# Where the mLSTM normalizer's column sum is made: on TensorE from four score tiles, or on VectorE first

## The chip, the cores and the metric

The kernel runs on one core of one Trainium2 chip. The metric is the device time of one execution in microseconds. The engines are named TensorE (PE, with its weight loads PEld), VectorE (DVE), ScalarE (ACT), GpSimd (POOL) and SyncE (SP, which starts the transfers).

## The reference, cut to what matters

Two transformer-like blocks run one after the other on 512 tokens of width 1024. The second block holds an mLSTM layer ("matrix memory") with 4 heads. In the kernel each head is computed over all 512 tokens at once and not chunk by chunk. For one head, with q and k of width 256 and v of width 512:

```
W[t, s]  = exp(F[t] - F[s] + i[s] - m[t])      for s <= t, else 0
Sm[t, s] = (q[t] . k[s]) * W[t, s]
num[t]   = sum over s of Sm[t, s] * v[s]
den[t]   = sum over s of Sm[t, s]
h[t]     = num[t] / max(|den[t]|, exp(-m[t]))
```

`den` is the normalizer. After it come an output gate, a layer norm over the 512 channels of the head, a skip term and a gate `silu(z)`, and then the output product.

## The kernel before, in words

All work is on tiles of 128 partitions by 512 tokens. Weights come in panels of 128 x 1024 through a ring of four buffers: SyncE loads `raw`, ScalarE rounds it to `w_hi` (line 1295), GpSimd computes `w_lo = raw - w_hi` (line 749). `dense` multiplies such a panel by a split input in three products (lines 778, 779, 784). The results go round the PSUM banks 0 to 3; tile t is in bank t % 4. `bank_ready(t)` makes TensorE wait until every earlier tile of that bank was taken, and `tile_taken(pe, t)` until tile t itself was. Banks 4 to 7 are for single sums and scores; `free` waits for one of them. Every engine works through its own instruction list in the order written, and semaphores join them. Nothing is scheduled at run time.

One head (`m_attend`) goes like this. The places that matter below are in this order on each engine.

- TensorE: products for q and k. Then v in two halves (lines 1079 to 1081), both halves into the tiles t0+4 to t0+7, which fill banks 0 to 3. Between the halves come the score products (line 1096), into banks 4, 5 and 6. After the second half of v comes the normalizer (line 1106): for each block n of 128 source tokens a product of a matrix of ones with the score tile `st` of that block, into bank 4. Block n only concerns the tokens from 128n on, so the four products have 512, 384, 256 and 128 columns. Then come the four numerator groups (line 1117, one for each 128 channels, d = 0 to 3) into the tiles t0+8 to t0+11, again banks 0 to 3, each with the same four widths. Then `dense(p0 + 4, t0 + 12)` for the first z tile, the product for the mean (line 1125), further z tiles, and the product for the variance (line 1131). The operands of lines 1096, 1106, 1117, 1125 and 1131 are plain fp32, and the trace holds two records for each such product.
- ScalarE: copies of q and k, the exponentials, the copies of the four v tiles to `mv` (line 1638), one panel rounding (line 1295), and then `den = |bank 4|` (line 1641). `den` is shown as `hf` in the trace.
- VectorE: the score tiles `st` (line 2233); then `max(den, exp(-m))` (line 2242), its reciprocal (line 2243), four products of it with the output gate `og` (line 2246), and four products of `og` with the numerator banks (line 2251). Each of the latter sets a numerator bank free. Between them the sum over channels is built up in `rstd` (lines 2255 and 2258). The mean product reads that sum.

The first numerator group has these two waits ahead of it:

```
bank_ready(t)
if d == 0:
    for n in range(NT):
        tile_taken(pe, t0 + 4 + n)
```

The tiles t0+4 to t0+7 are the v tiles, which ScalarE takes at line 1638.

Of the kernel before, what the change touches and what calls it, by code (L numbers as in the profile page):

```python
# [20 lines left out]
ALU = mybir.AluOpType  # L21
ACT = mybir.ActivationFunctionType

P = 128
S = 512
NT = S // P
# [188 lines left out]
def two_blocks(nc, A, out, stop=None):  # L215
    ctx = ExitStack()
    with ctx:
        def sem(name):
            return ctx.enter_context(nc.semaphore(name))
# [25 lines left out]
        ones = sb("ones", [P, P], F32)  # L245
# [7 lines left out]
        rstd = sb("rstd", [P, S], F32)  # L253
# [83 lines left out]
        st = sb("st", [P, 1280], F32, a)  # L337
# [69 lines left out]
        bank = [ctx.enter_context(nc.psum_tensor(f"bank{b}", [P, S], F32)) for b in range(8)]  # L407
# [102 lines left out]
        st_made = sem("st_made")  # L510
        den_done = sem("den_done")
        num_done = sem("num_done")
        absden_made = sem("absden_made")
        hsum_made = sem("hsum_made")
        msq_used = sem("msq_used")
        mean_done = sem("mean_done")
# [238 lines left out]
        def _(pe):  # L755
# [90 lines left out]
            for g in range(GG):  # L846
                mm = pe.transpose(bank[7][:, g * P:(g + 1) * P], ws[:, g, :], ident[:])
# [210 lines left out]
            def m_attend(i):  # L1058
                def free(b, n):
                    aux_released(pe, b, AUX_M[b] + n + i * M_AUX[b])  # L1060
                p0, t0 = M_BP[i], M_BT[i]
                for z in range(2):
                    dense(p0 + z, t0 + 2 * z, hi=xc_hi, lo=xc_lo, kt=4, width=2,
                          need=(lambda k: pe.wait_ge(xcs_made, i * MT + (k + 1))) if z == 0 else None)

                for z in range(2):
                    p = p0 + 2 + z
                    panel_split(pe, p)
                    if z == 0:
                        pe.wait_ge(xm_made, (i + 1) * MT)  # L1070
                    for n in range(NT):
                        if z == 0:
                            bank_ready(t0 + 4 + n)
                        dst = bank[(t0 + 4 + n) % RING][:, z * 256:(z + 1) * 256]
                        c = slice(n * P, (n + 1) * P)
                        for k in range(MT):
                            wh = w_hi[:, p % RING, k * 256:(k + 1) * 256]
                            wl = w_lo[:, p % RING, k * 256:(k + 1) * 256]
                            pe.matmul(dst, xm_hi[:, k, c], wh, start=(k == 0), stop=False, skip_group_check=True)  # L1079
                            pe.matmul(dst, xm_hi[:, k, c], wl, start=False, stop=False, skip_group_check=True)  # L1080
                            mm = pe.matmul(dst, xm_lo[:, k, c], wh, start=False, stop=(k == MT - 1),  # L1081
                                           skip_group_check=True)
                    mm.then_inc(panel_done[p % RING], 1)
                    if z == 0:

                        for e in range(MQ):
                            tile_taken(pe, t0 + e)
                            tile_taken(pe, t0 + 2 + e)
                        free(4, 0)
                        free(5, 1)  # L1090
                        free(6, 0)
                        for n in range(NT):
                            b, at = score_bank(n)
                            width = S - n * P
                            for e in range(MQ):
                                mm = pe.matmul(b[:, at:at + width], mk[:, e, n * P:(n + 1) * P],  # L1096
                                               mq[:, e, n * P:S], start=(e == 0 and n != 3), stop=(e == MQ - 1),
                                               skip_group_check=True)
                            mm.then_inc(scores_done, 1)

                place_st = [0, 512, 896, 1152]
                free(4, 1)
                for n in range(NT):
                    pe.wait_ge(st_made, i * NT + (n + 1))
                    w = S - n * P
                    mm = pe.matmul(bank[4][:, n * P:S], ones[:], st[:, place_st[n]:place_st[n] + w],
                                   start=(n == 0), stop=(n == NT - 1), skip_group_check=True)
                mm.then_inc(den_done, 1)
                for d in range(MT):
                    t = t0 + 8 + d  # L1110
                    bank_ready(t)
# [4 lines that stand above are left out]
                        w = S - n * P  # L1116
                        mm = pe.matmul(bank[t % RING][:, n * P:S], mv[:, n, d * P:(d + 1) * P],  # L1117
                                       st[:, place_st[n]:place_st[n] + w], start=(n == 0), stop=(n == NT - 1),
                                       skip_group_check=True)
                    mm.then_inc(num_done, 1)  # L1120

                dense(p0 + 4, t0 + 12)
                free(5, 2)
                pe.wait_ge(hsum_made, (i + 1) * (MT - 1))
                pe.matmul(bank[5][:], ones_m[:], rstd[:], start=True, stop=True).then_inc(mean_done, 1)
                dense(p0 + 5, t0 + 13)
                if i < MH - 1:
                    dense(p0 + 6, t0 + 14)
                free(6, 1)
                pe.wait_ge(msq_used, (i + 1) * MT)  # L1130
                pe.matmul(bank[6][:], ones_m[:], rstd[:], start=True, stop=True).then_inc(var_done, 1)
                if i == MH - 1:
                    dense(p0 + 6, t0 + 14)
                dense(p0 + 7, t0 + 15)
# [648 lines left out]
        def _(dve):  # L1783
# [430 lines left out]
            def m_attend(i):  # L2214
# [22 lines left out]
                dve.wait_ge(st_made, (i + 1) * NT)  # L2237
                for b in (4, 5, 6):
                    dve.sem_inc(aux_free[b], 1)

                dve.wait_ge(aux_free[4], AUX_M[4] + 2 + i * 2)
                link(dve.tensor_tensor(den, den, enm, ALU.max))
# [4 lines left out]
                for d in range(MT):  # L2247
                    t = t0 + 8 + d
                    dve.wait_ge(num_done, i * MT + (d + 1))
                    dve.wait_ge(den_used, i * MT + (d + 1))  # L2250
                    dve.tensor_tensor(og[:, d, :], bank[t % RING][:], og[:, d, :], ALU.mult)\
                       .then_inc(taken[t % RING], 1)
                    tile_taken(dve, t)
                    if d == 1:
                        dve.tensor_tensor(rstd[:], og[:, 0, :], og[:, 1, :], ALU.add).then_inc(hsum_made, 1)
                    elif d:
                        dve.wait_ge(hsum_made, i * (MT - 1) + (d - 1))
                        dve.tensor_tensor(rstd[:], rstd[:], og[:, d, :], ALU.add).then_inc(hsum_made, 1)
# [273 lines left out]
```

## Time and profile before

| | |
|---|---|
| median of 3 runs | 1710.41 us (1708.61 to 1710.64) |
| the profiled execution | 1710.67 us, span in the trace 1709.0 us |
| mean granted TensorE clock | 0.986 of full speed |
| TensorE busy | 1661.2 us, 97% of the span |
| VectorE, ScalarE, GpSimd busy | 864.2, 823.9, 715.2 us |
| chain that ended last | PE 87%, DVE 7%, ACT 4% |
| the four heads' normalizer products | first at 998.1 us, last head's at 1386.6 us |

Times in the trace count from the start of the span. A row of a timeline has the start, the length, the engine, the line and what was written from what; equal neighbours are merged with their count. A bracket says how long the engine had been idle before and what ended that. TensorE's records overlap, because a product begins before the one ahead of it has drained; so the distance between two starts is the cost of a product, and its record's length is more than that.

### The profile page before, as it was taken

To read this page: it belongs to the slowest core of one execution; us is meant where nothing else is said; L and a number is where in the kernel's file an instruction comes from. 1 tells how busy PE (TensorE), PEld (TensorE's weight loads), DVE (VectorE), ACT (ScalarE), POOL (GpSimd) and SP (SyncE) were. 2 spreads that over 40 slices of the span, in tenths; PEclk is the share of its full clock that TensorE was granted. 3 is DMA by queue.
4 is the path that set the end of the run, shared out by engine and by line. 5 is a ranking of instruction groups with operands and counts; after the bars stand their busy time and mean duration, and the time that the engine had idled before them with its cause. 6 is when DMAs were issued, how large, how long until landed. Compare 5 with 4: busy or idle time off the path is not lost.

```text
span 1709.0 us, 21678 instructions
## 1 busy us (share of the span) xinstructions
PE 1661.2 (97%) x7693; PEld 1362.4 (80%) x7693; DVE 864.2 (51%) x1356; ACT 823.9 (48%) x1091; POOL 715.2 (42%) x933
## 2 busy tenths in 40 slices
PE   6989999989999999999999999999999998999997
PEld 5878888878888888888887777877877876788875
DVE  4466666641113311111145757457447447688676
ACT  5366777653334423222246645445434435665664
POOL 5542333326666555555566535635635632000000
PEclk8989999999999999999999999999999999999999
DMA  6322212213333333333333222322422412322311
GB/s 175 99 62 62 61 49 61 62 38 93 99 104 99 99 99 98 94 96 96 98 98 90 72 60 75 111 62 75 111 61 68 116 52 79 97 88 66 107 56 59
DMA packets 251095, 142.94 MB, mean 84 GB/s; under 512 B 6161, under 2 KB 249618, under 8 KB 251026
## 3 DMA queue, kind: packets, MB, share of 16 engines
q1 hardware_dynamic: 251026, 142.00, 28.9%
q8 instruction: 45, 0.74, 0.2%
q14 instruction: 24, 0.20, 0.0%
HBM read 139.89 MB, written 2.10 MB: 83 GB/s over the span
## 4 chain that ended last, share of the span: by engine, by line
PE 87%; DVE 7%; ACT 4%; issue 1%; DMA 0%; SPq 0%; DVEq 0%; ACTq 0%
PE bank L778 22%; PE bank L779 22%; PE bank L784 22%; PE bank L1117 2%; PE bank L903 2%; PE bank L769 2%; PE bank L771 2%; PE bank L770 2%; ACT w_hi L1295 1%; PE bank L1096 1%; PE bank L1081 1%; PE bank L1080 1%; PE bank L1079 1%; PE bank L916 1%; DVE xT L2054 1%
## 5 line engine op out<-in xcount | busy, mean ns | idle before, releaser
L749 POOL TENSOR_TENSOR w_lo<-raw,w_hi 128x256 fp32r<-128x256 f32 x896 | 704.7, 819 | 711.6 <-ACT w_hi L1295 711.5
L1295 ACT ACTIVATE w_hi<-raw 128x1024 fp32r<-128x1024 f32 x264 | 277.5, 1056 | 538.2 <-PE bank L784 479.8
L778 PE MATMUL bank<-h_hi,w_hi 128*128 128x512 f32 x1252 | 501.3, 400 | 0.0
L779 PE MATMUL bank<-h_lo,w_hi 128*128 128x512 f32 x1252 | 490.1, 391 | 0.0
L784 PE MATMUL bank<-h_hi,w_lo 128*128 128x512 f32 x1252 | 309.3, 389 | 0.0
L778 PEld LDWEIGHTS bank<-h_hi,w_hi 128*128 128x128 f32 x1252 | 236.5, 189 | 56.3 <-issue 7.5
L779 PEld LDWEIGHTS bank<-h_lo,w_hi 128*128 128x128 f32 x1252 | 236.6, 189 | 52.8 <-issue 4.3
L784 PEld LDWEIGHTS bank<-h_hi,w_lo 128*128 128x128 f32 x1252 | 235.0, 188 | 48.8
L2054 DVE TENSOR_TENSOR xT<-xT,bank 128x512 f32<-128x512 f32 x103 | 68.3, 685 | 208.1 <-PE bank L784 156.9
L2079 DVE SCALAR_TENSOR_TENSOR fr<-bank,rstd 128x512 f32<-128x512 f32 x32 | 22.1, 692 | 133.6 <-PE bank L784 127.9
L778 PE MATMUL bank<-f_hi,w_hi 128*128 128x512 f32 x224 | 87.1, 389 | 0.0
L779 PE MATMUL bank<-f_lo,w_hi 128*128 128x512 f32 x224 | 87.1, 389 | 0.0
L2038 DVE TENSOR_TENSOR gated<-sg,bank 128x512 f32<-128x512 f32 x16 | 11.0, 689 | 110.3 <-PE bank L784 108.8
L903 PE MATMUL bank<-qk 128*128 128x64 f32 x448 | 56.1, 286 | 8.5 <-ACT vT L1396 8.5
L1380 ACT ACTIVATE ee<-ee 128x512 f32<-128x512 f32 x72 | 44.6, 630 | 37.0 <-DVE ee L1952 35.7
L903 PEld LDWEIGHTS bank<-qk 128*128 128x128 f32 x448 | 54.8, 203 | 9.5 <-issue 6.9
L784 PE MATMUL bank<-f_hi,w_lo 128*128 128x512 f32 x224 | 55.3, 389 | 0.0
L779 PEld LDWEIGHTS bank<-f_lo,w_hi 128*128 128x128 f32 x224 | 42.1, 188 | 8.8
L784 PEld LDWEIGHTS bank<-f_hi,w_lo 128*128 128x128 f32 x224 | 42.0, 188 | 8.7
L778 PEld LDWEIGHTS bank<-f_hi,w_hi 128*128 128x128 f32 x224 | 42.0, 188 | 8.7
L2331 DVE TENSOR_TENSOR w_lo<-raw,w_hi 128x1024 fp32r<-128x1024 f32 x40 | 48.7, 1217 | 0.0
L1998 DVE COPY_PREDICATED sd<-mask,bank 128x256 f32<-128x256 uint8 x56 | 29.5, 527 | 27.4 <-PE bank L903 21.5
(415 smaller groups left out, 2705.3 us busy)
## 6 DMA issues: line engine op xcount, KB each, us to landing
raw<-in_w_ff SPq DMA_DIRECT2D x64, 512.0 KB, 4.1
raw<-in_w_in SPq DMA_DIRECT2D x56, 512.0 KB, 3.8
raw<-in_m_w_in SPq DMA_DIRECT2D x48, 512.0 KB, 3.9
raw<-in_r_w_in SPq DMA_DIRECT2D x24, 512.0 KB, 3.9
raw<-in_m_w_out SPq DMA_DIRECT2D x16, 512.0 KB, 3.5
raw<-in_r_w_out SPq DMA_DIRECT2D x16, 384.0 KB, 3.1
raw<-in_w_up_b SPq DMA_DIRECT2D x8, 512.0 KB, 4.2
raw<-in_w_out SPq DMA_DIRECT2D x8, 512.0 KB, 4.2
```

The lines of the kernel that those rows point to most:

```text
L749: ins = pool.tensor_tensor(w_lo[:, s, part], raw[:, s, part], w_hi[:, s, part].bitcast(F32), ALU.subtract)
L769: pe.matmul(dst, w_hi[:, s, c], hi[:, k, :], start=(k == 0), stop=False)
L770: pe.matmul(dst, w_hi[:, s, c], lo[:, k, :], start=False, stop=False)
L771: mm = pe.matmul(dst, w_lo[:, s, c], hi[:, k, :], start=False, stop=(k == kt - 1))
L778: pe.matmul(dst, w_hi[:, s, c], hi[:, k, :], start=(k == 0), stop=False)
L779: pe.matmul(dst, w_hi[:, s, c], lo[:, k, :], start=False, stop=False)
L784: mm = pe.matmul(dst, w_lo[:, s, c], hi[:, k, :], start=False, stop=(k == kt - 1))
L903: mm = pe.matmul(dst, qk[:, m - 1, c], right, start=True, stop=True, skip_group_check=True)
L1295: act.activation(w_hi[:, p % RING, :], raw[:, p % RING, :], ACT.Copy).then_inc(hi_ready[p % RING], 1)
L1380: act.activation(ee[:, l % 3, :], ee[:, l % 3, :], ACT.Exp).then_inc(decay_made, 1)
L2054: dve.tensor_tensor(xT[:, j, :], xT[:, j, :], bank[t % RING][:], ALU.add).then_inc(taken[t % RING], 1)
L2331: dve.tensor_tensor(w_lo[:, q, :], raw[:, q, :], w_hi[:, q, :].bitcast(F32), ALU.subtract).then_inc(lo_ready[q], 1)
```

## The change

On VectorE, once the four score tiles are made, three additions put the tiles n = 1, 2 and 3 together with tile 0 for the tokens from 128 on (384, 256 and 128 columns) and write the sum to `rstd`, a buffer that is free at that point. They sit ahead of `max(den, ...)` in VectorE's list.

On TensorE the four products with ones go away. Two take their place: one over the 128 columns of tile 0 that no other tile reaches, and one over the 384 columns of `rstd`. These two stand behind the first numerator group (d = 0) and no longer ahead of it. TensorE now waits for all four score tiles at once, and for the three additions ahead of the two products.

VectorE gets one further wait, for `den_done`, ahead of its first channel sum, since that one overwrites `rstd`.

```diff
--- before.py
+++ after.py
@@ -510,7 +510,7 @@
         st_made = sem("st_made")
         den_done = sem("den_done")
         num_done = sem("num_done")
-        absden_made = sem("absden_made")
+        stsum_made = sem("stsum_made")
         hsum_made = sem("hsum_made")
         msq_used = sem("msq_used")
         mean_done = sem("mean_done")
@@ -1099,13 +1099,7 @@
                             mm.then_inc(scores_done, 1)
 
                 place_st = [0, 512, 896, 1152]
-                free(4, 1)
-                for n in range(NT):
-                    pe.wait_ge(st_made, i * NT + (n + 1))
-                    w = S - n * P
-                    mm = pe.matmul(bank[4][:, n * P:S], ones[:], st[:, place_st[n]:place_st[n] + w],
-                                   start=(n == 0), stop=(n == NT - 1), skip_group_check=True)
-                mm.then_inc(den_done, 1)
+                pe.wait_ge(st_made, (i + 1) * NT)
                 for d in range(MT):
                     t = t0 + 8 + d
                     bank_ready(t)
@@ -1118,6 +1112,12 @@
                                        st[:, place_st[n]:place_st[n] + w], start=(n == 0), stop=(n == NT - 1),
                                        skip_group_check=True)
                     mm.then_inc(num_done, 1)
+                    if d == 0:
+                        free(4, 1)
+                        pe.wait_ge(stsum_made, (i + 1) * (NT - 1))
+                        pe.matmul(bank[4][:, 0:P], ones[:], st[:, 0:P], start=True, stop=False, skip_group_check=True)
+                        pe.matmul(bank[4][:, P:S], ones[:], rstd[:, P:S], start=False, stop=True,
+                                  skip_group_check=True).then_inc(den_done, 1)
 
                 dense(p0 + 4, t0 + 12)
                 free(5, 2)
@@ -2237,6 +2237,12 @@
                 dve.wait_ge(st_made, (i + 1) * NT)
                 for b in (4, 5, 6):
                     dve.sem_inc(aux_free[b], 1)
+                dve.tensor_tensor(rstd[:, P:S], st[:, P:S], st[:, place_st[1]:place_st[1] + S - P],
+                                  ALU.add).then_inc(stsum_made, 1)
+                for n in range(2, NT):
+                    dve.wait_ge(stsum_made, i * (NT - 1) + (n - 1))
+                    dve.tensor_tensor(rstd[:, n * P:S], rstd[:, n * P:S], st[:, place_st[n]:place_st[n] + S - n * P],
+                                      ALU.add).then_inc(stsum_made, 1)
 
                 dve.wait_ge(aux_free[4], AUX_M[4] + 2 + i * 2)
                 link(dve.tensor_tensor(den, den, enm, ALU.max))
@@ -2252,6 +2258,7 @@
                        .then_inc(taken[t % RING], 1)
                     tile_taken(dve, t)
                     if d == 1:
+                        dve.wait_ge(den_done, i + 1)
                         dve.tensor_tensor(rstd[:], og[:, 0, :], og[:, 1, :], ALU.add).then_inc(hsum_made, 1)
                     elif d:
                         dve.wait_ge(hsum_made, i * (MT - 1) + (d - 1))
```

## Rows read from the trace of the kernel before

**Rows 1.** The page: busy time of each engine, and the chain that ended last.
```profile
PE 1661.2 (97%) x7693; PEld 1362.4 (80%) x7693; DVE 864.2 (51%) x1356; ACT 823.9 (48%) x1091; POOL 715.2 (42%) x933
...
PE 87%; DVE 7%; ACT 4%; issue 1%; DMA 0%; SPq 0%; DVEq 0%; ACTq 0%
```

**Rows 2.** Timeline, TensorE, head 0: start us, length us, engine, line, operation, tiles, [idle].
```profile
997.98 0.28 PE L1081 MATMUL bank<-w_hi,xm_lo 128*128 128x256 f32 x1
998.10 2.32 PE L1106 MATMUL bank<-st,ones 128*128 128x512 f32 x8
1000.50 8.87 PE L1117 MATMUL bank<-st,mv 128*128 128x512 f32 x32
...
1014.82 0.59 PE L1125 MATMUL bank<-rstd,ones_m 128*128 128x512 f32 x1
```

**Rows 3.** Timeline, ScalarE, head 0.
```profile
998.29 2.06 ACT L1638 ACTIVATE mv<-bank 128x512 f32<-128x512 f32 x4 [4.39 <-PE bank L1081]
1000.22 1.08 ACT L1295 ACTIVATE w_hi<-raw 128x1024 fp32r<-128x1024 f32 x1
1001.17 0.62 ACT L1641 ACTIVATE hf<-bank 128x512 f32<-128x512 f32 x1
```

**Rows 4.** Timeline, TensorE's weight loads, head 0.
```profile
1003.60 1.49 PEld L1117 LDWEIGHTS bank<-st,mv 128*128 128x128 f32 x7 [0.24 <-issue]
...
1005.76 1.49 PEld L1117 LDWEIGHTS bank<-st,mv 128*128 128x128 f32 x7 [0.24 <-issue]
...
1009.23 0.19 PEld L778 LDWEIGHTS bank<-h_hi,w_hi 128*128 128x128 f32 x1
```

**Rows 5.** Timeline, VectorE, head 0.
```profile
992.61 0.62 DVE L2233 TENSOR_TENSOR st<-ww,bank 128x256 f32<-128x256 f32 x2 [0.37 <-PE bank L1096]
1001.82 0.83 DVE L2242 TENSOR_TENSOR hf<-hf 128x512 f32<-128x512 f32 x1 [8.59 <-ACT hf L1641]
...
1008.49 1.41 DVE L2251 TENSOR_TENSOR og<-bank,og 128x512 f32<-128x512 f32 x2
...
1012.59 0.69 DVE L2258 TENSOR_TENSOR rstd<-rstd,og 128x512 f32<-128x512 f32 x1
```

**Rows 6.** Waits from 975 to 1500 us: waiter, releaser, us, times, longest.
```profile
DVE hf L2242 <- ACT hf L1641: 34.4, 4, 8.6
...
ACT mv L1638 <- PE bank L1081: 17.6, 4, 4.4
```

**Rows 7.** Groups by shape, VectorE, 950 to 1500 us: busy us, mean ns, idle.
```profile
L2288 DVE TENSOR_TENSOR og<-og,rstd 128x512 f32<-128x512 f32 x16 | 15.0, 938 | 0.1
...
L2233 DVE TENSOR_TENSOR st<-ww,bank 128x384 f32<-128x384 f32 x4 | 2.2, 554 | 0.9 <-PE bank L1096 0.9
```

**Rows 8.** Timeline, GpSimd, head 0.
```profile
1001.38 3.23 POOL L749 TENSOR_TENSOR w_lo<-raw,w_hi 128x256 fp32r<-128x256 f32 x4 [4.58 <-ACT w_hi L1295]
```

**Rows 9.** Stretches: us; busy us (instructions) of PE, PEld, DVE, ACT, POOL; clock; DMA.
```profile
1422.90:1424.80 1.90, 0.00 (x0) 0.00 (x0) 1.81 (x3) 0.62 (x2) 0.00 (x0) 1.00 0.00 0
1425.00:1428.00 3.00, 3.00 (x8) 2.10 (x8) 2.93 (x4) 1.39 (x2) 2.17 (x3) 0.51 0.09 25
...
967.73:969.64 1.91, 1.91 (x6) 0.66 (x5) 1.91 (x3) 1.71 (x3) 1.91 (x4) 1.00 0.20 37
971.10:974.40 3.30, 3.30 (x9) 2.55 (x8) 3.30 (x4) 2.70 (x4) 3.30 (x4) 0.50 0.49 128
1054.80:1056.70 1.90, 1.90 (x5) 0.66 (x4) 1.83 (x4) 0.14 (x1) 0.00 (x0) 1.00 0.04 9
1057.00:1060.40 3.40, 3.40 (x16) 2.78 (x16) 3.26 (x6) 2.29 (x4) 1.52 (x2) 1.00 0.00 0
```

**Rows 10.** Timeline, TensorE, head 3.
```profile
1410.86 1.10 PE L1131 MATMUL bank<-rstd,ones_m 128*128 128x512 f32 x2 [1.01 <-DVE rstd L2284]
```

## The prediction

> **What bounds the kernel now.** I read the page first. TensorE is busy 97% of the span and carries 87% of the chain that ended last [rows 1]. So work taken off TensorE looks like time won, and that is the case for this change. But a share over the whole span hides what ends each wait in the stretch that is edited, so I went on to the timelines of one head, engine by engine. The four heads repeat each other: the wait of ScalarE for the v products and the wait of VectorE for the normalizer each occur four times, at 17.6 / 4 = 4.4 us and 34.4 / 4 = 8.6 us [rows 6].
>
> In TensorE's timeline [rows 2] the last v product ends at 998.26 (997.98 + 0.28), the normalizer runs from 998.10 to 1000.42, and the numerator begins at 1000.50. It looks like one unbroken stream. ScalarE's timeline tells what it hides: the four v copies start at 998.29, when the last v product has ended, and end at 1000.35 [rows 3]. By the code the first numerator group waits for all four copies. It starts 0.15 us after the last of them. So the start of the numerator is set by ScalarE, and the old normalizer fills exactly the 2.24 us (998.26 to 1000.50) in which TensorE has nothing else that it may do. Its cost on TensorE is close to nothing.
>
> The second thing to see is who waits for the normalizer. ScalarE copies it at 1001.17, directly behind a panel rounding that began at 1000.22 [rows 3]. It was complete at 1000.42, so it was ScalarE's list that held the copy. VectorE had been idle for 8.59 us when the copy released it at 1001.82. From there its list runs to 1012.59 + 0.69 without a pause [rows 5]. In that list the first numerator bank is set free at 1009.19 (the two records of line 2251 take 1.41 us together from 1008.49, so one takes 0.70). TensorE's next step, the first z tile, needs that bank, and its weight load starts at 1009.23 [rows 4]. TensorE and VectorE meet there within 0.04 us. VectorE's list has no slack at this point, and it is the normalizer that starts the list.
>
> **The change part by part.**
>
> *Products removed and put in.* A numerator group has the same four widths as the old normalizer and takes 1005.76 - 1003.60 = 2.16 us [rows 4]. That is ten blocks of 128 columns. The new pair has 128 + 384 columns, four blocks: 2.16 x 4 / 10 = 0.86 us. Nominal saving: 1.30 us a head, 5.2 us for four. None of it is on the path: what is removed lay under the v copies (they end at 1000.35 whatever TensorE does), and what is put in lies behind the first group, where nothing covers it. So TensorE's own list gets 0.86 us longer between 1000.50 and the z tile: it would arrive at 1009.23 + 0.86 = 1010.09.
>
> At this place the Trainium skill has a rule that speaks against the change (TensorE: Matmul & The Clock Gate, Part 2, Step-by-step): only weight loads are pulled ahead; the products themselves stay in program order. By it TensorE can't do the new pair during the 2.24 us, although its operands are there. If it could, the normalizer would be ready as early as now and the time would stay near the old one.
>
> *The additions on VectorE.* The trace has no addition of 384, 256 or 128 columns from SBUF alone. From below: the score tile of 384 columns takes 0.55 us [rows 7], so three shorter or equal ones take at most 1.7 us at that rate. From above: a 512-column product of two SBUF tiles takes 0.94 us on average where other engines are at work [rows 7], three take 2.8 us. They start at 993.23, when the last score tile is done [rows 5], and end between 994.9 and 996.1. TensorE asks for them at about 1002.7. The cover is 6.6 us or more, inside an idle stretch of 8.59 us; I take nothing. GpSimd may work at the same time; even if all three additions held it up in full, 2.8 us fit into its idle 4.58 us ahead of its next split [rows 8]. No transfer and no queue of SyncE is touched. The additional wait of VectorE for `den_done` comes after work that itself needed the normalizer, so it is always met: nothing.
>
> *The wait for all four score tiles at once.* They are done at 993.23, 5 us before TensorE gets there: nothing.
>
> *The move.* This is what costs. Now: the normalizer's last product ends at 1000.42 and the copy starts at 1001.17. After: the first numerator group starts at 1000.50 as before, the pair begins at 1002.66, its stream ends at 1003.52, and the last record drains 0.16 us later (as 2.32 stands to 2.16 in the old group), at 1003.68. ScalarE has nothing in its list between the rounding and this copy, and starts 0.03 us after, as it does with the v copies (998.26, 998.29). So the copy starts at 1003.71: 2.54 us later. All of VectorE's list behind it moves by the same. The first numerator bank comes free at 1009.19 + 2.54 = 1011.73, and TensorE, there since 1010.09, waits 1.68 us for it. The z tile starts at 1011.77, 2.54 us late. The mean product has no new wait: now the sum is ready at 1013.28 and TensorE arrives at 1014.82 [rows 2, 5]; both move by 2.54. Everything behind follows from TensorE or VectorE and moves along. Bounds: the pair may cost up to 0.1 us more for its short products, and ScalarE's step down to 0; 2.5 to 2.65 us a head. For four heads: 4 x 2.54 = 10.2 us.
>
> *TensorE's clock.* After the change TensorE stands still from 998.26 to 1000.50, 2.24 us, in each head. What the clock does after such a stop can be read in the last head's output. TensorE did nothing for 1.90 us at full clock, and then the granted clock was 0.51, near 1.2 GHz, where it had been 2.4 GHz [rows 9]. The second stop of this kind (2.05 us) is followed by the same. The four pairs of products with only four rows, 1.9 us each, which is almost a stop, went two ways: behind the first (967.73) the clock was 0.50, behind the second (1054.80) it stayed 1.00 [rows 9]; the third is like the first and the fourth like the second. So four of six such stretches brought a low stretch. One lasts a little over the 3.3 us of its row, in which 9 products were done and not 16, and costs about half its length, 1.7 us. Here the low stretch would lie over the first numerator group and the pair, 3.18 us from the start to the end of the pair. All of that is now on the path to VectorE, so there is no cover. If it begins late, only part counts (3.18 - 2 = 1.2 us if it begins 2 us behind the start); I take 1.5 us. Four of six, for four heads: 2.7 low stretches, 4.0 us. The new 1.68 us wait could bring such stretches too, at 1.7 us each; the nearest rows are 1.90 us (low after) and 1.01 us (no low row after it) [rows 10]. I take none and keep two in the upper bound.
>
> The Trainium skill (the same page, Part 1, What's actually happening, and HAM oscillation) says that a throttled gate is the default state, that work releases it and idling brings it back, and that the penalty is the low time multiplied by one minus the granted share. By that the low stretch costs half of itself, which agrees with 9 against 16 products in rows 9. Without any clock effect the sum would be 10.2 us, with it 14.2.
>
> **Sum.** The profiled execution took 1710.67 us around a span of 1709.0. 1710.67 + 10.2 + 4.0 = 1724.9 us. It lies 0.26 us above the median of the runs, so against the median: 1710.41 + 14.2 = 1724.6 us, 0.8% slower.
>
> **The rivals.** A measurement of this kernel can tell about 0.2% (3.4 us) from no change.
>
> A. *The move alone, with the clock holding* (none or one low stretch): +10.2 to +11.7 us, 1720.6 to 1722.1. For it: two of six stretches kept full clock. Against it: both real stops lost it.
>
> B. *Low clock nearly everywhere*: all four stops (+6.0), and two of the four waits ahead of the z tile (+3.4): 10.2 + 9.4 = +19.6, 1730.0 us.
>
> C. *The z tile isn't held by VectorE.* If the bank were free well before 1009.23, the late list would be absorbed and only the uncovered pair would count: 4 x 0.86 = +3.4 us, 1713.9. Against it: the 0.04 us between bank and weight load in rows 4 and 5.
>
> D. *Faster: TensorE's arithmetic sets the pace.* Then the 1.30 us saved per head arrive in full: -5.2 us, 1705.2. It needs the numerator to be able to start before 1000.35, that is, the v copies not to be what it waits for. The point that decides is where the first record of line 1117 stands against the end of the copies. For it: 97% busy, and no wait for the copies is listed between the old normalizer and the numerator. Against it: 0.15 us between the end of the copies and the start, and two waits in the code.
>
> **How the numbers follow.** The forecast with two or three low stretches has 0.58, A 0.17, B and what lies between 0.15, C 0.06, D 0.04. The forecast's own range is 1722 to 1727. With A and most of B the range is 1719 to 1730; it leaves out C, D and the end of B. C ends just at the edge of the 0.2%, so I put half of it at no change. Faster 0.04, same 0.03, slower 0.93.
>
> **What the profile after would show.** A stop of TensorE of about 2.2 us ahead of the first record of line 1117 in each head, with the release by ScalarE's v copies. The normalizer's copy about 5.4 us behind the start of the v copies and not 2.9. Three additions inside the idle stretch of VectorE, and nothing that waits for them. A stop of about 1.7 us before the first z product, released by line 2251. A clock of 0.5 behind two or three of the four first stops. I would be wrong if the numerator began at once after v, if the z tile started without a wait, or if the low stretches came more or less often than counted.

## The result and the profile after

The changed kernel takes 1727.12 us (median of 4 runs, 1726.17 to 1728.19) against 1709.62 for the kernel before, measured beside it (1708.61 to 1710.64). The ratio is 1.0104, interval 1.0089 to 1.0119: 17.5 us slower. The profiled execution took 1727.80 us with a span of 1726.1. Run again later, the same kernel gave 1723.14 (1720.97 to 1726.32) against 1710.41, ratio 1.0084, interval 1.0070 to 1.0098: 12.7 us slower. The spread between the two is dealt with below.

The page of the changed kernel, busy times and the chain that ended last (answers to [rows 1]):

```profile
PE 1664.4 (96%) x7677; PEld 1365.4 (79%) x7677; DVE 873.1 (51%) x1368; ACT 823.9 (48%) x1091; POOL 713.0 (41%) x933
...
PE 80%; DVE 10%; ACT 6%; issue 3%; DMA 0%; ACTq 0%; DVEq 0%; SPq 0%
```

TensorE is busy 3.2 us longer, although it does fewer products. Its share of the chain fell from 87% to 80%, and ScalarE and VectorE took over. Two new entries stand in the list of TensorE's waits, the first of them at its top (us in total, times, longest):

```profile
PE bank L1111 <- ACT mv L1638: 9.0, 4, 2.2
...
PE bank L778 <- DVE og L2257: 5.8, 4, 1.5
```

Neither of the two was in the list before. One head, the second, at full clock (it answers to [rows 2]):

```profile
1136.90 2.40 PE L1111 MATMUL bank<-st,mv 128*128 128x512 f32 x8 [2.25 <-ACT mv L1638]
1139.13 0.39 PE L1118 MATMUL bank<-st,ones 128*128 128x128 f32 x2
1139.35 0.81 PE L1119 MATMUL bank<-rstd,ones 128*128 128x384 f32 x2
1140.00 6.64 PE L1111 MATMUL bank<-st,mv 128*128 128x512 f32 x24
1148.10 0.50 PE L778 MATMUL bank<-h_hi,w_hi 128*128 128x512 f32 x1 [1.46 <-DVE og L2257]
```

The numerator group d = 0 begins after 2.25 us of nothing, released by the v copies. The pair takes 1140.00 - 1139.13 = 0.87 us. The z product begins after 1.46 us of nothing, released by VectorE's taking of the first numerator bank. ScalarE in the same head (answers to [rows 3]):

```profile
1134.69 2.06 ACT L1638 ACTIVATE mv<-bank 128x512 f32<-128x512 f32 x4 [4.39 <-PE bank L1081]
1136.61 1.08 ACT L1295 ACTIVATE w_hi<-raw 128x1024 fp32r<-128x1024 f32 x1
1140.20 0.60 ACT L1641 ACTIVATE hf<-bank 128x512 f32<-128x512 f32 x1 [2.51 <-PE bank L1119]
```

From the first v copy to the normalizer's copy it is 1140.20 - 1134.69 = 5.51 us; before it was 1001.17 - 998.29 = 2.88 [rows 3]. VectorE (answers to [rows 5]):

```profile
1129.01 0.62 DVE L2233 TENSOR_TENSOR st<-ww,bank 128x256 f32<-128x256 f32 x2 [0.36 <-PE bank L1096]
1129.96 0.56 DVE L2240 TENSOR_TENSOR rstd<-st 128x384 f32<-128x384 f32 x1 [0.33 <-DVE st L2233]
1130.55 1.59 DVE L2244 TENSOR_TENSOR rstd<-rstd,st 128x256 f32<-128x256 f32 x2
1140.83 0.69 DVE L2248 TENSOR_TENSOR hf<-hf 128x512 f32<-128x512 f32 x1 [8.69 <-ACT hf L1641]
...
1147.36 1.41 DVE L2257 TENSOR_TENSOR og<-bank,og 128x512 f32<-128x512 f32 x2
```

The three additions are done at 1132.14, 7.0 us before TensorE uses them. Then the list waits 8.69 us for the normalizer, and the first bank is free at 1147.36 + 0.70 = 1148.06, 0.04 us before the z product begins.

The best measure of the edited stretch is the distance from the first v copy to the first z product: 1148.10 - 1134.69 = 13.41 us, where it was 1009.23 - 998.29 = 10.94 before [rows 3, 4]. Taken from unrounded starts it is 10.93 in each of the four heads before, and 13.41 in three heads after; the first head has 15.10. So 2.48 us a head come from the order of the work, 9.9 us in all.

The rest of the difference is TensorE's clock. Stretches of the changed kernel (columns as in [rows 9], the clock is the third number from the end):

```profile
1002.40:1005.60 3.20, 3.20 (x6) 1.48 (x6) 0.00 (x0) 0.54 (x1) 2.58 (x4) 0.50 0.02 5
...
1063.80:1067.10 3.30, 3.30 (x9) 2.65 (x8) 3.19 (x4) 1.32 (x2) 2.42 (x3) 0.50 0.02 5
1136.90:1140.00 3.10, 3.10 (x12) 2.04 (x13) 0.00 (x0) 0.79 (x1) 2.23 (x4) 1.00 0.01 2
...
1196.90:1200.20 3.30, 3.30 (x9) 2.56 (x8) 3.20 (x4) 1.22 (x3) 2.74 (x3) 0.50 0.00 0
1330.10:1333.30 3.20, 3.20 (x9) 2.43 (x9) 3.13 (x4) 1.11 (x3) 2.77 (x3) 0.50 0.00 0
```

The first lies on the numerator and the pair of the first head: 15.10 - 13.41 = 1.69 us. The second, fourth and fifth lie behind the casts of the second, third and fourth head (so the code calls two products ahead of v, lines 1037 and 1039, that use only four rows of TensorE). Between the z product of one head and the first v copy of the next it is 118.05 us at full clock and 119.65 with such a stretch; before, that happened once in three, here three times: 2 x 1.6 = 3.2 us. The first v copy of the first head comes at 999.94 and not 998.29, also by the clock: from 374 to 377 us the granted clock is 0.50 in this execution and 1.00 in the one before. Nothing that runs ahead of that point was changed. The last part, from the fourth head's z product, is 0.6 us longer; in the last head's output the clock is 0.53 over 11 us (1442 to 1453) and was 0.70 before (1424 to 1435). The sum: 9.9 + 1.7 + 3.2 + 1.6 + 0.6 = 17.0, of 17.1 between the spans.

### The profile page after: what moved, and what is told of

Read it like the earlier page. It is cut to its first block, busy times and chain, and to the rows that moved or that the text cites. A ratio compares the mean times of both kernels' runs of the same rounds, so it can differ in the third digit from the quotient of the medians.

```text
span 1726.1 us, 21666 instructions
## 1 busy us (share of the span) xinstructions
PE 1664.4 (96%) x7677; PEld 1365.4 (79%) x7677; DVE 873.1 (51%) x1368; ACT 823.9 (48%) x1091; POOL 713.0 (41%) x933
## 4 chain that ended last, share of the span: by engine, by line
PE 80%; DVE 10%; ACT 6%; issue 3%; DMA 0%; ACTq 0%; DVEq 0%; SPq 0%
PE bank L778 21%; PE bank L779 21%; PE bank L784 20%; PE bank L769 2%; PE bank L770 2%; PE bank L771 2%; PE bank L903 2%; ACT w_hi L1295 2%; PE bank L1096 1%; DVE ee L1952 1%; PE bank L1081 1%; PE bank L1080 1%; PE bank L1079 1%; DVE qk L1967 1%; DVE qk L1966 1%
## 5 line engine op out<-in xcount | busy, mean ns | idle before, releaser
L1111 PE MATMUL bank<-st,mv 128*128 128x512 f32 (+3 forms) x128 | 37.8, 451 | 9.0 <-ACT mv L1638 9.0
```

## The experiments

In all tables "z" is the distance from the first v copy to the first z product, at full clock. "Before" is the kernel before, measured on the same chip in the same session. Rows are from a timeline of all engines in one head.

**The pair in the old place.** The additions and the pair stay, only the place is undone:

```diff
-                pe.wait_ge(st_made, (i + 1) * NT)
+                free(4, 1)
+                pe.wait_ge(stsum_made, (i + 1) * (NT - 1))
+                pe.matmul(bank[4][:, 0:P], ones[:], st[:, 0:P], start=True, stop=False, skip_group_check=True)
+                pe.matmul(bank[4][:, P:S], ones[:], rstd[:, P:S], start=False, stop=True,
+                          skip_group_check=True).then_inc(den_done, 1)
                 for d in range(MT):
...
-                    if d == 0:
-                        free(4, 1)
-                        pe.wait_ge(stsum_made, (i + 1) * (NT - 1))
-                        pe.matmul(bank[4][:, 0:P], ones[:], st[:, 0:P], start=True, stop=False, skip_group_check=True)
-                        pe.matmul(bank[4][:, P:S], ones[:], rstd[:, P:S], start=False, stop=True,
-                                  skip_group_check=True).then_inc(den_done, 1)
```

> The additions on VectorE and the pair of products as in the change, but the pair stands ahead of the first numerator group, where the four products stood. Theory (the move costs, because the normalizer comes late to ScalarE and VectorE): the pair ends inside the 2.24 us of the v copies, the normalizer's copy starts where it started before (2.9 us behind the first v copy), the z product waits for nothing, and the time is the old one, 1709 to 1711 us. If the clock falls after the stop of about 1.4 us that is left, 1.7 us more each time. Rival (the additions on VectorE or the second operand in rstd cost): the time stays near 1727. Rival D of the prediction (TensorE's columns are the time): 5.2 us below the kernel before, 1705.

Measured: 1710.28 us against 1710.49, ratio 0.9998 (0.9988 to 1.0007).

```profile
1127.76 2.07 ACT L1636 ACTIVATE mv<-bank 128x512 f32<-128x512 f32 x4 [4.39 <-PE bank L1081]
1127.79 0.81 PE L1105 MATMUL bank<-rstd,ones 128*128 128x384 f32 x2
...
1129.97 8.87 PE L1115 MATMUL bank<-st,mv 128*128 128x512 f32 x32 [1.38 <-ACT mv L1636]
...
1130.63 0.62 ACT L1639 ACTIVATE hf<-bank 128x512 f32<-128x512 f32 x1
...
1138.69 0.50 PE L778 MATMUL bank<-h_hi,w_hi 128*128 128x512 f32 x1
```

z is 10.93 in all four heads, as before. The numerator now begins after 1.38 us of nothing, 2.21 us behind the first v copy, and ScalarE copies the normalizer 2.87 us behind it. The additions cost nothing, and the 1.30 us a head that TensorE no longer works brought nothing. The loss comes with the place, and not with the additions or the second operand in `rstd`. This falsifies rival D.

**The move alone.** The kernel before, its four products put behind the first group, no additions:

```diff
-                free(4, 1)
-                for n in range(NT):
-                    pe.wait_ge(st_made, i * NT + (n + 1))
...
-                mm.then_inc(den_done, 1)
+                pe.wait_ge(st_made, (i + 1) * NT)
                 for d in range(MT):
...
                     mm.then_inc(num_done, 1)
+                    if d == 0:
+                        free(4, 1)
+                        for n in range(NT):
+                            w = S - n * P
+                            mm = pe.matmul(bank[4][:, n * P:S], ones[:], st[:, place_st[n]:place_st[n] + w],
+                                           start=(n == 0), stop=(n == NT - 1), skip_group_check=True)
+                        mm.then_inc(den_done, 1)
```

> The kernel before with one edit: its four products with ones stand behind the first numerator group. No additions on VectorE. Theory: the normalizer comes 2.16 us late instead of 0.86 us behind the first group, so 1.30 us a head more than the change: 4 x 1.30 = 5.2 us slower than the changed kernel, about 1732 us. The z product waits as long as in the changed kernel (1.5 us), because TensorE and VectorE are both 1.30 us later. Rival (the z product's wait isn't on the path): as the change. Low-clock stretches can move either by 1.7 us each.

Measured: 1727.50 us (1722.33 to 1730.82) against 1710.49, ratio 1.0091 (1.0068 to 1.0114).

```profile
1133.01 2.06 ACT L1639 ACTIVATE mv<-bank 128x512 f32<-128x512 f32 x4 [4.39 <-PE bank L1081]
...
1137.45 2.32 PE L1119 MATMUL bank<-st,ones 128*128 128x512 f32 x8
...
1139.81 0.60 ACT L1642 ACTIVATE hf<-bank 128x512 f32<-128x512 f32 x1 [3.80 <-PE bank L1119]
...
1147.70 0.50 PE L778 MATMUL bank<-h_hi,w_hi 128*128 128x512 f32 x1 [1.46 <-DVE og L2252]
```

z is 14.70 us from unrounded starts, in the two heads at full clock; that is 1.29 more than in the changed kernel, as the four products take 1139.61 - 1137.45 = 2.16 us (the next numerator group starts at 1139.61), 1.29 more than the pair; the wait at z is 1.46 us in both. So the term was as expected. The median was not, 1727.5 and not 1732: 4 x (14.70 - 10.93) = 15.1 us are direct, 17.0 were measured, and the four runs spread over 8.5 us. The two shorter ones (1722.33 and 1724.54) had a mean granted clock of 0.988 and 0.986, the two longer ones (1730.46 and 1730.82) 0.983 and 0.984.

**The first bank earlier.** The changed kernel, with another order on VectorE:

```diff
-                for d in range(MT):
-                    dve.wait_ge(o_made, i * MT + (d + 1))
-                    dve.tensor_tensor(og[:, d, :], og[:, d, :], den, ALU.mult).then_inc(den_used, 1)
+                by_den(0)
                 for d in range(MT):
+                    if d + 1 < MT:
+                        by_den(d + 1)
                     t = t0 + 8 + d
```

`by_den(d)` holds the two lines that the loop had.

> The changed kernel with VectorE's list in another order: the reciprocal is multiplied into the output gate for d = 0 and 1, then numerator 0 is taken, then d = 2, numerator 1 and so on, instead of all four first. The first bank comes free two products earlier (2 x 0.61 = 1.2 us). Theory (the z product is held by that bank): its wait falls from 1.46 us to about 0.3, and the time by up to 4 x 1.2 = 4.7 us, to 1722 to 1723; the mean product may then wait for the channel sum, which isn't earlier, and give up to half of it back. Rival C (the z product isn't held): no change, 1727.

Measured: 1714.95 us (1712.81 to 1719.33) against 1710.49, ratio 1.0037 (1.0023 to 1.0052).

```profile
1258.38 2.06 ACT L1638 ACTIVATE mv<-bank 128x512 f32<-128x512 f32 x4 [4.39 <-PE bank L1081]
...
1263.89 0.60 ACT L1641 ACTIVATE hf<-bank 128x512 f32<-128x512 f32 x1 [2.51 <-PE bank L1119]
...
1269.84 0.69 DVE L2260 TENSOR_TENSOR og<-bank,og 128x512 f32<-128x512 f32 x1
...
1270.58 0.50 PE L778 MATMUL bank<-h_hi,w_hi 128*128 128x512 f32 x1 [0.26 <-DVE og L2260]
```

The bank is taken 11.46 us behind the first v copy, z begins at 12.20 and waits 0.26 us: 1.21 us a head won, 4.8 in all. That excludes rival C: the z product is held by this bank. The mean product didn't wait for its sum. The median fell by 12 us against the first measurement of the changed kernel and by 8 against its second; the part above 4.8 goes with the clock (mean granted 0.985 to 0.989 here, 0.981 to 0.983 and 0.982 to 0.986 there). The profiled execution shows where: one low stretch on a numerator (the second head's z is 13.88 us), and none behind the casts, where the changed kernel had three. Why they stayed away isn't shown.

**The stop filled.** The changed kernel, with the four old products also run ahead of the numerator; the pair overwrites their result:

```diff
-                pe.wait_ge(st_made, (i + 1) * NT)
+                free(4, 1)
+                for n in range(NT):
+                    pe.wait_ge(st_made, i * NT + (n + 1))
+                    w = S - n * P
+                    mm = pe.matmul(bank[4][:, n * P:S], ones[:], st[:, place_st[n]:place_st[n] + w],
+                                   start=(n == 0), stop=(n == NT - 1), skip_group_check=True)
                 for d in range(MT):
...
                     if d == 0:
-                        free(4, 1)
                         pe.wait_ge(stsum_made, (i + 1) * (NT - 1))
```

> The changed kernel with the four old products with ones put back ahead of the numerator as well, their result being overwritten by the pair; they fill the stop of 2.24 us with work and set no time otherwise. Theory: the late normalizer is untouched, so 4 x 2.47 = 9.9 us above the kernel before stays; no low clock on the first numerator group in any head, so at most the one low stretch (1.7 us) of the changed kernel is won: 1719.5 to 1726, the upper part if low stretches elsewhere stay. Rival (the stop itself costs, by the clock): the time falls by more than 4 us and the low stretches behind the casts and in the last head's output go too.

Measured: 1723.17 us (1720.79 to 1724.96) against 1710.49, ratio 1.0075 (1.0058 to 1.0092).

```profile
1131.45 2.32 PE L1106 MATMUL bank<-st,ones 128*128 128x512 f32 x8
1131.65 2.06 ACT L1642 ACTIVATE mv<-bank 128x512 f32<-128x512 f32 x4 [4.39 <-PE bank L1081]
...
1145.06 0.50 PE L778 MATMUL bank<-h_hi,w_hi 128*128 128x512 f32 x1 [1.46 <-DVE og L2261]
```

TensorE no longer stops ahead of the numerator, and z is the same 13.41 us in all four heads. So the stop in itself isn't the direct loss; what counts is that the normalizer comes late. No head had a low stretch on its numerator. Behind the casts two of three still had one. The median is 4.0 us below the first measurement of the changed kernel and the same as its second (1723.14), so no gain from filling the stop is shown.

**One v copy for each product.** The pair ahead as in the first experiment, and the first group waits copy by copy:

```diff
-                    if d == 0:
-                        for n in range(NT):
-                            tile_taken(pe, t0 + 4 + n)
                     for n in range(NT):
+                        if d == 0:
+                            tile_taken(pe, t0 + 4 + n)
```

> The pair ahead of the first numerator group, and each of that group's four products waits only for its own v copy, not for all four. The numerator then starts about 1.4 us earlier (with the first copy, behind the pair). Theory (VectorE's list, started by the normalizer's copy on ScalarE, holds the first bank until 10.9 us behind the first v copy): the z product starts where it did, 10.93 us behind the first v copy, TensorE only waits in another place, and the time is that of the kernel before, 1710. Rival (TensorE's list is the bound once the copies don't hold it): z 1.4 us earlier in each head, 5.5 us in all, 1705.

Measured: 1710.66 us against 1710.66, ratio 1.0002 (0.9993 to 1.0011).

```profile
1125.71 2.07 ACT L1635 ACTIVATE mv<-bank 128x512 f32<-128x512 f32 x4 [4.39 <-PE bank L1081]
...
1126.45 8.87 PE L1114 MATMUL bank<-st,mv 128*128 128x512 f32 x32
...
1128.58 0.62 ACT L1638 ACTIVATE hf<-bank 128x512 f32<-128x512 f32 x1
...
1136.64 0.50 PE L778 MATMUL bank<-h_hi,w_hi 128*128 128x512 f32 x1 [1.32 <-DVE og L2254]
```

The numerator begins 0.74 us behind the first v copy and not 2.21, and all of it is given back: z waits 1.32 us and stands at 10.93 again. In the kernel before, TensorE and VectorE reach this point within 0.1 us of each other, and easing TensorE alone brings nothing. VectorE alone wasn't eased in any run; by the same 0.1 us it could not give much.

**Both eased.** As the last, and in addition the VectorE order of the third experiment, and on ScalarE:

```diff
-                upper(p0 + 3 + RING)
                 act.wait_ge(den_done, i + 1)
                 act.activation(den, bank[4][:], ACT.Abs).then_inc(aux_free[4], 1)
+                upper(p0 + 3 + RING)
```

> As the copy-by-copy kernel, and two orders are changed: ScalarE copies the normalizer ahead of the panel rounding (0.9 us earlier), and VectorE takes numerator 0 after two of its four products with the reciprocal (1.2 us earlier). The first bank is then free before TensorE comes. Theory: z starts when TensorE has done the pair and the numerator without a stop, 0.86 + 8.64 = 9.5 us behind the first v copy and not 10.93: 1.4 us a head, 5.7 us, 1704 to 1705. Low-clock stretches can move it by 1.7 us each. Rival (something else holds z or the mean product): no more than 2 us gained.

Measured: 1704.51 us (1702.76 to 1705.24) against 1710.66, ratio 0.9965 (0.9951 to 0.9978). It is the fastest version of this study.

```profile
1125.88 2.06 ACT L1635 ACTIVATE mv<-bank 128x512 f32<-128x512 f32 x4 [4.39 <-PE bank L1081]
...
1126.62 8.87 PE L1114 MATMUL bank<-st,mv 128*128 128x512 f32 x32
...
1127.80 0.63 ACT L1637 ACTIVATE hf<-bank 128x512 f32<-128x512 f32 x1
...
1133.79 0.68 DVE L2257 TENSOR_TENSOR og<-bank,og 128x512 f32<-128x512 f32 x1
...
1135.24 0.47 PE L778 MATMUL bank<-h_hi,w_hi 128*128 128x512 f32 x1
```

The normalizer's copy stands 1.92 us behind the first v copy, the bank is free at 8.59, and z begins without a wait at 9.37: 1.56 us a head less than before, 6.2 us, and the medians differ by 6.15. How much of it each of the two new orders brings wasn't separated.

**The same with four products.** The last kernel's waits and orders put on the kernel before:

> The same waits and orders as the kernel above, but with the normalizer as in the kernel before: four products on TensorE, no additions on VectorE. Theory: the four products take 2.16 us, 1.30 more than the pair, and the numerator starts at about 2.2 us behind the first copy; z 10.7 us behind it, 0.2 to 0.3 earlier than before, 1709. The difference to the kernel above, 4 x 1.2 to 1.3 = 5 us, is what the additions on VectorE are worth where they stand in the clear. Rival (adding on VectorE gives nothing anywhere): both kernels alike.

Measured: 1710.26 us (1707.17 to 1710.63) against 1710.66, ratio 0.9996 (0.9987 to 1.0005).

```profile
1128.52 2.06 ACT L1637 ACTIVATE mv<-bank 128x512 f32<-128x512 f32 x4 [4.39 <-PE bank L1081]
...
1130.47 8.80 PE L1116 MATMUL bank<-st,mv 128*128 128x512 f32 x32
...
1136.63 0.68 DVE L2253 TENSOR_TENSOR og<-bank,og 128x512 f32<-128x512 f32 x1
...
1139.03 0.48 PE L778 MATMUL bank<-h_hi,w_hi 128*128 128x512 f32 x1
```

z is 10.51 us, 0.42 less than before, and without a wait. The numerator begins 1.95 us behind the first v copy, held by the four products. The kernel with the additions is 10.51 - 9.37 = 1.14 us a head ahead, 4.6 us; the medians differ by 5.75. Here the additions pay what the change wanted of them. The expected 1709 was missed by 1.3 us; its 1.7 us of direct gain do not show against a clock that was 0.984 to 0.987 in its runs.

**A longer head.** The changed kernel with the variance product issued twice (the first result is overwritten):

```diff
+                pe.matmul(bank[6][:], ones_m[:], rstd[:], start=True, stop=True)
                 pe.matmul(bank[6][:], ones_m[:], rstd[:], start=True, stop=True).then_inc(var_done, 1)
```

> The changed kernel with the variance product done twice (the first result is overwritten), 0.86 us more of TensorE in each head, so the heads no longer follow each other at 133.1 us, the spacing at which the low-clock stretches behind the casts stood. If those stretches only add up by chance of where the stages fall, fewer of them come, and the time rises by less than 3.4 us or falls. If they belong to the change itself, all stay and the time is 1727 + 3.4 = 1730.5.

Measured: 1726.63 us (runs 1731.70, 1723.73, 1729.53, 1723.03) against 1710.66, ratio 1.0091 (1.0074 to 1.0108). The runs fall in two pairs: 1723.0 and 1723.7 with a clock of 0.986 and 0.985, 1729.5 and 1731.7 with 0.982 and 0.981. The first pair is near what the direct terms give: 1710.7 + 9.9 + 3.4 = 1724.0. So the low clock beyond the usual comes and goes from run to run of one and the same kernel. The experiment didn't decide its question: the median rose by less than 3.4 us, as the first reading expected, but the profiled execution, the longest run, kept all three stretches behind the casts and had two more on numerators.

**The changed kernel again.**

> The changed kernel, unaltered, to see how its time spreads. Of its 17 us, 9.9 are the four heads' late z product (13.41 against 10.93 us behind the first v copy) and 1.7 one low-clock stretch on a numerator group; 5.5 are low stretches elsewhere, 1.6 of them ahead of the first head, where nothing was changed. If these last fall by chance, some runs come at 1722 to 1724 and the mean granted clock varies from 0.981 to 0.986. If the change brings them each time, all runs stay at 1726 to 1728 with a clock of 0.981 to 0.983.

Measured: 1723.14 us (1720.97, 1724.84, 1722.88, 1723.14, 1726.32) against 1710.41. The fastest run had a clock of 0.985, the slowest 0.982. The profiled one, the fastest, has z at 13.41 in all four heads, no low stretch on a numerator, and one behind each of the three casts; its first v copy comes at 996.46 and not at 999.94. So the loss that is there each time is the 9.9 us, and much of the rest comes and goes, as the first reading expected; the stretches behind the casts stayed even in the fastest run. At the kernel before's usual clock (0.985, 0.986) the runs lie at 1721.0 to 1723.1; the direct term gives 1710.4 + 9.9 = 1720.3.

**Behind the group, with everything eased.** The waits and orders of the fastest kernel, the pair behind the first numerator group:

> The three eased waits and orders (copy by copy, normalizer ahead of the rounding, numerator 0 taken early), but with the pair behind the first numerator group, as the change has it. Theory: the numerator starts with the first v copy (0.7 us behind its start), the normalizer's copy at about 4.0 us behind it and not 1.92 as with the pair ahead, the first bank is free 6.7 us after that, z at 10.7 to 10.8, so about the time of the kernel before, 1709 to 1710. The place alone then costs 10.75 - 9.37 = 1.4 us a head, 5.5 us, against the same kernel with the pair ahead (1704.5). Rival (the place no longer matters once the waits are eased): 1704 to 1705.

Measured: 1709.97 us (1706.94 to 1712.05) against 1710.41, ratio 1.0004 (0.9995 to 1.0013).

```profile
1255.51 2.07 ACT L1637 ACTIVATE mv<-bank 128x512 f32<-128x512 f32 x4 [4.39 <-PE bank L1081]
...
1256.26 2.39 PE L1110 MATMUL bank<-st,mv 128*128 128x512 f32 x8 [0.78 <-ACT mv L1637]
...
1259.56 0.60 ACT L1639 ACTIVATE hf<-bank 128x512 f32<-128x512 f32 x1 [1.98 <-PE bank L1118]
...
1266.25 0.50 PE L778 MATMUL bank<-h_hi,w_hi 128*128 128x512 f32 x1 [0.26 <-DVE og L2259]
```

z is 10.74 us, against 9.37 with the pair ahead: the place costs 1.37 us a head, 5.5 in all, and the medians differ by 5.46 (they come from two sessions; each taken against its own kernel before, it is 5.7). Even with everything eased it takes back what the additions bring.

## Why the prediction was right

The forecast was 1724.6 us, 14.2 us slower, with a range of 1719 to 1730; measured were 1727.1 (17.5 us slower, 0.1 us above the forecast's own 1722 to 1727) and, again, 1723.1 (12.7 slower). The late normalizer, the larger term, was right by its mechanism. That the total came as close was partly luck: the clock's term was mis-sized and stood in the wrong place. Step by step:

- *The v copies hide the old normalizer.* Right. The stop it leaves is 2.25 us, predicted 2.24. The pair in the old place changes nothing.
- *The pair costs 0.86 us behind the first group.* Right: 0.87. The move alone shows the other 1.29 us.
- *The additions are covered.* Right: they take 2.18 us from the first start to the last end and end 7.0 us before their use, and with the pair ahead the time is the old one.
- *The late normalizer is on the path, 2.54 us a head.* Right in place, 2.48 in size. The normalizer's copy came 0.09 us later than worked out, mostly since the first group takes 2.23 us and not 2.16 after a stop; in return `max(den, ...)` took 0.69 us and not 0.83 (before, GpSimd's split ran beside it [rows 8]; after, that split had ended 0.29 us earlier; whether that is the cause wasn't tested). The wait at z was 1.46 us and not 1.68.
- *Low clock on the numerator.* The mechanism was right: where it happens, z moves by 1.69 us. The count was wrong. I put four of six, 2.7 of four heads; it was one of four in this profile and none of four when profiled again. By the prediction's own sign of being wrong, stretches more or less often than counted, this step failed. Over the five profiled executions that have the stop it is 6 of 20 (the change 1 and again 0, the move alone 2, the first bank earlier 1, the longer head 2). By that rate the term is 2 us and not 4.
- *Nothing of the clock elsewhere.* The sum has no such term and gives no reason. In the first measurement this was wrong, and it made up for the last. In the profiled execution 5.5 us of the loss come from low stretches on work that the change doesn't touch; 1.6 of them ahead of the first head. So the term of the sum that was mis-sized is the clock's: 4.0 predicted, all on the stops; 1.7 on the stops and 5.5 elsewhere found.

By the count of low stretches on the stops (one, then none) it was rival A that happened, and not the forecast's two or three; of the times only the fastest run of the second measurement (1720.97) lies in rival A's 1720.6 to 1722.1, since the low clock elsewhere adds to it. Rivals C and D are excluded, as the experiments say. Rival B didn't occur: behind 20 waits of 1.46 us at the z product, in five profiled executions, no low stretch followed.

The Trainium skill (TensorE: Matmul & The Clock Gate, Part 1, What's actually happening) says that idling brings the throttled state back. The traces agree that it can, but for stops of 2.25 us it was 6 of 20, so by the rows it is a risk and not a fixed price.

What stays open is the stretches behind the casts. All three profiled executions of the changed kernel and of the longer head had them in three of three heads, the kernel before and the kernel with the pair ahead in one of three. But the first bank earlier, which has the late pair and the stops too, had none, and "both eased", which has neither, had two. In the changed kernel the stretches begin 133.1 us apart (1063.8, 1196.9, 1330.0), and the heads also follow each other at 133.1 us. Whether the two belong together, or the count is chance, was not settled.

## What to carry to other kernels

Work on the busiest engine may be free if it stands where the engine would wait anyway; before it is shortened or moved, look for what the next instruction waits for besides it. Moving a producer behind other work costs the consumer's whole list, even if the producer itself is cheap: here 0.87 us of products, put behind a group of 2.23 us, became 2.48 us of delay. When two engines meet at a point within a tenth of a microsecond, look at both before easing one: TensorE alone gave 0.0 us, both gave 6.2.

## What the hardware showed unexpectedly

Products with only four rows in use (1.9 us of them) were followed by half clock in 0 to 3 of the second to fourth head, 21 of 36 over the twelve profiled executions, though TensorE is busy throughout in the trace; behind the 2.25 us stops it was 6 of 20. Two measurements of one kernel, each against the kernel before in the same session, differed by 4.8 us (17.5 and 12.7), and the runs of single kernels by up to 8.7 us; the mean granted clock of a run (0.981 to 0.989) goes with it. For a change worth 10 us the distance between two events in one head at full clock (10.93, 13.41, 9.37 us, the same to 0.01 in every head) told more than the medians.
